# Eight products of the rounded weights, then eight of the remainders: the order inside a half unit

## The reference

```
# first block
h = rms_norm(x);  proj = h @ w_in            # 2048 x 8192, eight parts of 1024
y_conv = rms_norm(short_gated_conv(...)) * silu(z_conv)
y_attn = rms_norm(causal attention, 8 heads of 128) * silu(z_attn)
x = x + concat([y_conv, y_attn]) @ w_out     # 2048 x 2048
# second block
mods = silu(c) @ w_ada + b_ada               # six vectors, for the tokens and for a context
q, k, v, u = split(modulate(rms_norm(x)) @ w_in_2)
x = x + g_a * (concat([window_attention(q, k, v, context), pool(u)]) @ w_out_2)
hm = modulate(rms_norm(x))
x = x + g_m * (square(relu(hm @ w_mlp_up)) @ w_mlp_down)     # 2048 x 8192 and back
out = rms_norm(x)
```

## Time and profile before

| | |
|---|---|
| time, median of 3 runs | 1883.11 us (1882.97 to 1885.88) |
| profiled execution: span | 1886.6 us |
| profiled execution's own time | not listed apart from the three; its span is 0.7 us above the longest of them |
| TensorE matmuls, busy | 1696.6 us, 90%, 9662 instructions |
| TensorE weight loads, busy | 1368.7 us, 73% |
| VectorE, busy | 1136.1 us, 60% |
| ScalarE, busy | 807.0 us, 43% |
| GpSimd, busy | 31.4 us, 2% |
| mean granted TensorE clock | 0.955 of full speed |
| HBM | 198 GB/s over the span |

### The profile page before, as it was taken

The page is one execution under the profiler, slowest core; times in us unless marked ns, Lnnn a source line. Parts: engine busy times, 40 slices in busy tenths (PEclk is TensorE's granted clock), DMA queues, the critical chain, the costliest instruction groups (busy, mean ns, idle before and its releaser), DMA issues.

```text
span 1886.6 us, 30937 instructions
## 1 busy us (share of the span) xinstructions
PE 1696.6 (90%) x9662; PEld 1368.7 (73%) x9662; DVE 1136.1 (60%) x1787; ACT 807.0 (43%) x1182; POOL 31.4 (2%) x48
## 2 busy tenths in 40 slices
PE   4899999999979887888789679899989998999896
PEld 2677777677756666656678558788878887888785
DVE  5455555566665557566666576556565555556675
ACT  5344444343434334444334434444444444444452
POOL 0000000000000000000000000000000000000000
PEclk9899999899989898999999879999999999999998
DMA  7677777677756764643235424555455554554452
GB/s 308 241 263 267 262 264 259 227 289 299 293 198 241 267 227 141 235 178 134 90 123 166 157 75 164 174 189 178 167 179 187 175 171 168 188 178 167 167 184 95
DMA packets 88330, 374.07 MB, mean 198 GB/s; under 512 B 10256, under 2 KB 10768, under 8 KB 75488
## 3 DMA queue, kind: packets, MB, share of 16 engines
q1 hardware_dynamic: 87120, 369.54, 56.0%
q0 software_dynamic: 1168, 4.00, 0.7%
HBM read 371.40 MB, written 2.10 MB: 198 GB/s over the span
## 4 chain that ended last, share of the span: by engine, by line
issue 73%; DVE 14%; PE 7%; ACT 4%; DVEq 1%; POOL 0%; ACTq 0%; POOLq 0%
DVE lo L981 5%; PE G L391 3%; ACT hi L695 2%; PE G L392 1%; PE M L596 1%; DVE sm L1263 1%; DVE t L981 1%; DVE blk L1276 1%; DVE blk L981 1%; ACT sq L849 1%; DVE W L981 1%; DVE sqsum L981 1%; ACT blk L910 1%; DVE blk L1284 1%; PE S L649 1%
## 5 line engine op out<-in xcount | busy, mean ns | idle before, releaser
L391 PE MATMUL G<-actA,hi 128*128 128x512 f32 x2368 | 869.7, 409 | 37.5 <-DVE actA L981 31.1
L981 DVE TENSOR_TENSOR lo<-raw,hi 128x1024 fp32r<-128x1024 f32 x496 | 607.8, 1225 | 360.4 <-ACT hi L695 318.8
L392 PE MATMUL G<-actA,lo 128*128 128x256 f32 x2368 | 669.0, 283 | 0.0
L695 ACT ACTIVATE hi<-raw 128x1024 fp32r<-128x1024 f32 x496 | 525.8, 1060 | 213.4 <-PE G L392 174.0
L391 PEld LDWEIGHTS G<-actA,hi 128*128 128x128 f32 x2368 | 451.5, 191 | 210.3 <-issue 61.2
L391 PE MATMUL G<-actB,hi 128*128 128x512 f32 x1536 | 562.6, 408 | 24.3 <-DVE actB L981 18.9
L392 PEld LDWEIGHTS G<-actA,lo 128*128 128x128 f32 x2368 | 454.3, 192 | 0.3
L392 PE MATMUL G<-actB,lo 128*128 128x256 f32 x1536 | 438.2, 285 | 0.0
L391 PEld LDWEIGHTS G<-actB,hi 128*128 128x128 f32 x1536 | 297.5, 194 | 114.9 <-DVE actB L981 21.3
L392 PEld LDWEIGHTS G<-actB,lo 128*128 128x128 f32 x1536 | 299.0, 195 | 0.2
L695 ACT ACTIVATE tmpB<-G 128x256 f32<-128x256 f32 x248 | 95.2, 384 | 339.2 <-PE G L392 326.5
(11 more groups left out here) (155 smaller groups left out, 831.7 us busy)
## 6 DMA issues: line engine op xcount, KB each, us to landing
raw<-stream_dram SPq DMA_DIRECT2D x496, 512.0 KB, 3.4
ada_raw<-w_ada_dram SPq DMA_DIRECT2D x96, 1024.0 KB, 6.2
x_tok<-x_tok_dram SPq DMA_DIRECT2D x1, 2048.0 KB, 7.7
resid<-xT_dram SPq DMA_DIRECT2D x1, 2048.0 KB, 10.4
ctx_tok<-ctx_tok_dram SPq DMA_DIRECT2D x1, 2048.0 KB, 17.9
W<-ctxT_dram POOLq DMA_DIRECT2D x16, 128.0 KB, 5.3
out_dram<-resid SPq DMA_DIRECT2D x4, 512.0 KB, 2.6
ada_raw<-pool_w_dram POOLq DMA_DIRECT2D x1, 1024.0 KB, 5.0
```

The source lines that it names most:

```text
L391: pe.matmul(bank[:], hi[:, slot, cols], x[:, k, :], start=(k == 0), stop=False, skip_group_check=True)
L392: m = pe.matmul(bank[:, 0:T], lo[:, slot, cols], x[:, k, 0:T], start=False, stop=(k == KT - 1), skip_group_check=True)
L695: return act.activation(dst, src, ACT.Copy)
L981: return dve.tensor_tensor(dst, a, b, op)
```

## The change

In `half_unit` the single loop becomes two. The first waits for `hi_done` in place of `lo_done` and issues the eight `hi` products; then comes the wait for `lo_done`, and the second loop issues the eight `lo` products. The waits for `ready` stay with the `hi` products. All else, the other engines' programs among it, is as before.

```
             def half_unit(at, j, half, x, ready=None, ready_base=0):
                 slot = (2 * j + half) % RING
-                pe.wait_ge(lo_done, at.unit(j, 1 + half, 2))
+                pe.wait_ge(hi_done, at.unit(j, 1 + half, 2))
                 if half == 0 and not (isinstance(at.i, int) and at.base + j < 2):
                     pe.wait_ge(evac_done, at.unit(j, -1))
                 bank = G[j % 2]
...
                     if ready is not None:
                         pe.wait_ge(ready, ready_base + k + 1)
                     cols = slice(n * P, (n + 1) * P)
-
                     pe.matmul(bank[:], hi[:, slot, cols], x[:, k, :], start=(k == 0), stop=False, skip_group_check=True)
+                pe.wait_ge(lo_done, at.unit(j, 1 + half, 2))
+                for n in range(KT // 2):
+                    k = half * KT // 2 + n
+                    cols = slice(n * P, (n + 1) * P)
                     m = pe.matmul(bank[:, 0:T], lo[:, slot, cols], x[:, k, 0:T], start=False, stop=(k == KT - 1),
                                   skip_group_check=True)
                 m.then_inc(w_used, 1)
```

## The result

The changed kernel takes 1893.95 us (median of 6 runs, 1892.57 to 1895.27), the kernel before beside it 1886.32 (6 runs, 1882.97 to 1890.91): ratio 1.0043, 95% interval 1.0027 to 1.0058. It is slower by 7.6 us by the medians. The profiled span grew by 5.7 us, from 1886.6 to 1892.3.

A forecast was written before the change was run, and what follows sets the result against it. TensorE bounds the down projections, a turn of ScalarE and VectorE the ends of the up projections. 3.0 us at four first down units plus 3.75 at five starts made 6.8, taking the median 1883.1 to 1889.9 us; range 1880.5 to 1897.

The forecast's parts named there:

- the ring: Ends of up projections: ScalarE and VectorE wait on each other in turn, 6.2 us a unit, TensorE in no step.
- Four first down units: First down unit after each up projection: seven slots deferred past the last tile cost 4 x 0.75 = 3.0 us.
- rival 4: Clock: if all four resumptions at half clock lasted as long as the longest, 5.4 us more, 1895; 0.12 with rival 5.
- (a): First unit, last tile at 39.14, full clock: deferred remainders cost 0.8 us.
- (b): First output projection, last tile at 559.90, half clock: 1.5 us more, 0.5 of it covered, so 0.95.
- (c): Key and value units, at 699.34: 0.8 us less 0.1 hidden by the sum of squares, so 0.7.
- (d): Switch to the latent tokens, 735.15, half clock: 1.5 us less 0.6 won back; 0.9 at half clock, 0.6 taken.
- (e): First up projection, 1108.81, mostly half clock: 1.4 us, half of it given back, so 0.7.
- Rival 1: At gated tiles the deferral costs next to nothing, the 6.8 us shrinking under 3.8: about 1885 us; chance 0.25.
- Rival 2: Early starts are passed on: at most 10.6 us of matmul idle comes back, less 6.8, giving 1879; chance 0.07.
- Rival 3: Runs of equal-size products stream faster, 0.17 us less per TensorE-bound half unit: -43 + 7, about 1847 us; chance 0.08.
- Rival 5: The stream falls into the slower of its two paces everywhere: +6 us, 1896; chance 0.12 together with rival 4.

The follow-up runs named there:

- the wait alone: Kernel before with only the wait moved to the rounding, products alternating as before: 1886.55 us, ratio 0.9992.
- the order alone: Kernel before with eight rounded products, then eight remainder products, both behind the wait for `lo_done`: 1894.23 us, ratio 1.0032.
- gated-only kernel: Changed order only in half units that wait for activations tile by tile, the kernel before's alternating order elsewhere: 1895.06 us, ratio 1.0037.
- rings sped up: Kernels where ScalarE rounds the next weights before the activation; against the kernel before, 0.9743 in up units only, 0.9524 in output projections too.
- all rings sped up: Kernel before with ScalarE rounding the next weights ahead of the activation in up units and both output projections: 1796.68 us, ratio 0.9524.

## Why the prediction was right

The sign held, and so did the mechanism: the order at gated tiles costs, and the moved wait gives nothing. The time lies in the range, 1 us above the 1887 to 1893 that had the most weight, and the kernel before was 3.2 us slower here than in the three executions on record then. By ratio, 0.36% was forecast and 0.43% measured. The sum came out better than its parts. By its steps:

- **The moved wait: 0.** Held. The matmuls' waits for `lo` vanished, the ring stayed at 6.2 us, and the wait alone gave 0.9992. The changed kernel and the grouped order without early starts lie 0.3 us apart by their medians.
- **The second wait: 0.** Held: it shows in no list, and the grouped order without it (the order alone) takes the same 2.793 us a half unit and the same time.
- **The order of the products: 0, with 6 us to either side.** The order fell into neither pace. It has one of its own, 2.793. That the two nearly cancel is luck: the profiled execution of the kernel before had the faster pace in two down projections and the slower in two, and others have another mix. Starts of half units against the kernel before: +0.56 us over each of the first two down projections (28 x 0.020), -0.9 over each of the last two (28 x 0.034). Sum -0.7.
- **Four first down units: 3.0.** The delay jumps by 1.5 us at each, which is 2.30 less 0.81, and part comes back while the lower level lasts. From the unit before to the end of the stretch +0.5, +1.6, +0.5 and +0.7 us: 3.4. The second is dearer, and there the lower level ended 5.0 us after the last tile, not 3.4 as before. At the other three it ended 0.1 to 0.8 us sooner than before (5.3, 4.8 and 4.7 us, where it was 6.1, 5.4 and 4.8), so rival 4 is true of one gate in four. Its price of 5.4 was too high as well: it took all four for as short as the shortest, and by these numbers it would have been 2.4.
- **Five starts: 3.75.** Each showed at its gate, and less of it stayed. (a) 0.9 us by the third half unit, as said (0.8), but all of it was back by half unit 20, behind a stretch at half clock that lasted 6.8 us instead of 10.2: net 0. (b) The evacuation came 0.9 us later (0.95); 0.6 was left at the end of the projection. (c) +0.6 (0.7). (d) +0.9 at once (0.6), but at unit 88, three units on, the delay was 0.3 us less than ahead of the gate. (e) +1.6, 1.1 of it kept (0.7). There is a sixth start that the prediction left out, the second output projection: +0.9, all given back within it. The starts kept some 2.0 us, not 3.75.
- **Not in the prediction: 1.9 us in the query and pool units,** where no tile is waited for. 1.6 of it came in one step, in the 3.4 us below, in which TensorE is busy throughout in both kernels and the granted clock is full before and half after:

```profile
790.60:794.00 3.40, 3.40 (x31) 2.32 (x28) 0.60 (x2) 0.38 (x1) 0.00 (x0) 1.00 0.99 416
```

```profile
790.60:794.00 3.40, 3.40 (x18) 1.83 (x16) 0.17 (x1) 0.38 (x1) 0.00 (x0) 0.50 1.00 424
```

The kernel with the wait alone makes the same step of 1.6 us there and loses nothing in all; the one with grouping only where nothing is gated doesn't make it. Whether the change causes it stays open.

The sum by the profiles, over the half units' starts: -0.8 up to the first output projection, +4.0 from there to the first MLP group with (b) to (e) and the query and pool units, +3.4, -0.7: 5.9, where the profiled spans differ by 5.7. The -0.8 can't be put down to the order: the kernel with the wait alone is 2.2 us ahead at the same place. My 6.8 lies between the 5.7 and the 7.6 us of the medians, but in part by luck, since the 1.9 us that I had not seen make up for what the starts gave back. What is shown without such a sum is that grouping the gated half units alone costs 7.0 us, against the 6.8 forecast for them.

Three gated starts, TensorE in the changed kernel, answer to the earlier trace rows:

```profile
39.61 1.12 PE L395 MATMUL G<-actA,lo 128*128 128x256 f32 x8
40.57 2.00 PE L390 MATMUL G<-actA,hi 128*128 128x512 f32 x8
...
699.15 0.50 PE L390 MATMUL G<-actC,hi 128*128 128x512 f32 x1 [1.22 <-DVE actC L984]
699.49 1.10 PE L395 MATMUL G<-actC,lo 128*128 128x256 f32 x8
700.42 0.50 PE L436 MATMUL S<-ones,sqsum 128*128 128x1 f32 x4
...
1111.51 1.91 PE L395 MATMUL G<-actA,lo 128*128 128x256 f32 x8
1113.21 1.05 PE L390 MATMUL G<-actA,hi 128*128 128x512 f32 x2
```

Behind the last tile at 699.15 the sum of squares follows after 1.27 us, 0.55 before; at the first up projection the eight remainders alone take 1.70 us.

Rival 1 (the deferral is free) falls with the gated-only kernel: all of the loss is there. Rival 2 falls with the ring at 6.2 us and with the wait alone at 0.9992. Rival 3 falls with the steady rows: a rounded product in a run of eight takes 1.84/8 = 0.230 us, as in alternation, a remainder 0.119. By the Trainium skill ("TensorE: Matmul & The Clock Gate", section "Back-to-back issue gap") they would be 0.216 and 0.109, by its formula for the isolated gap of a single product; the measurement decides, and the excess over the page's figure is not the price of mixing sizes. The prediction also gave line 649's 0.216 us in favour of this rival. Those products have 256 columns, where a rounded product has 512, so that row says nothing for it; a remainder product, with 256 columns too, takes 0.12. Rival 5, the slower pace everywhere, falls with 2.793.

What I would not have said before: on five sixths of its half units the change is free or a small gain (0.9985), and the loss is on the rest. And its size depends on what bounds the kernel. Where TensorE never waits for the last tile, the deferral at the four first down units costs nothing. Where nothing but TensorE bounds the MLP, the pace counts in all of its 256 half units: the grouped order is 5.1 us slower there than an execution at 2.773 and 8.6 us faster than one at 2.827, and the profiles show either in alternating kernels with the rings sped up.

## What to carry to other kernels

Ask of a wait what comes late if it goes: 53 us of waiting were worth nothing, since TensorE stood in none of the steps of the ring, and one swap of two ScalarE instructions in that ring was worth 50. Where operands come one by one and the engine waits for them, finish all that each one allows before waiting for the next; work put off past the last of them lands on the path, here at half clock. Where the operands are there in time, the same order cost nothing at these places. An order that is good where operands are ready and bad where they trickle in can be chosen place by place.

## What was unexpected in the hardware

- The same alternating instructions run at two paces, 2.773 and 2.827 us a half unit, each steady over a whole down projection; the grouped ones at 2.793 in every profile. In the profiles the pace of alternating products in the MLP changes only at a first down unit with its stall, and where no stall is left it is one pace through all 256 half units: 2.773 in two kernels with rings sped up, 2.827 in the third. What chooses between the two stays open. It isn't which weights, since the same down projections run at either. The times fit this: 29 executions of the kernel before spread over 11.8 us, 11 of the order alone over 2.0. Other causes of that spread are not excluded.
- After the same stall of 4.1 us, the lower clock lasted 3.4 us in one group of the kernel before and 6.1 in another. Time at it was 172.1 us before, 189.0 after and 110.6 with all rings sped up, in one profiled execution each. Of the 6.6 to 7.9 us that the first two down units of a group gained without the stall, 4.1 were the stall. The half clock behind it lasted 3.4 to 6.1 us and so cost an estimated 1.7 to 3.1, half its length, which is most of the rest.
